# Streaming-encoder trunk on one core: statistics and transposes of q, k, v a slot later, last slab released by VectorE, high part of h by ScalarE

## What is computed

```python
def rms_norm(x, g):
    return x * lax.rsqrt(jnp.mean(x * x, axis=-1, keepdims=True) + EPS) * g

def odd_mixer(h, w_qkv, q_norm_g, k_norm_g, w_out):      # layer 1, 8 heads of 128
    q, k, v = jnp.split(h @ w_qkv, 3, axis=-1)
    q, k = rms_norm(q, q_norm_g), rms_norm(k, k_norm_g)  # per head
    o = stick_breaking(q, k, v)
    return o @ w_out

# per block of 128 queries, for all keys up to its end, mask: key < query
    z = q @ k.T * scale
    log_keep = where(mask, log_sigmoid(-z), 0)
    acc = cumsum(log_keep, reverse=True) - log_keep
    w = where(mask, exp(log_sigmoid(z) + acc), 0);  o = w @ v

# each layer l
    h = rms_norm(x, norm_mix_g[l]) * (1 + sc1) + sh1
    x = x + g1 * (even_mixer(h) if l % 2 == 0 else odd_mixer(h))
    h = rms_norm(x, norm_ffn_g[l]) * (1 + sc2) + sh2
    x = x + g2 * ((silu(h @ w_gate) * (h @ w_up)) @ w_down)
```

## Time and profile before

| | us |
|---|---|
| median of 3 runs | 2844.98 |
| the three runs | 2829.68, 2845.26, 2844.98 |
| the profiled execution | 2835.24 |
| its span (first to last instruction) | 2833.4 |
| PE busy in it | 2606.2 (92%) |
| DVE, ACT, POOL busy | 1412.3, 500.2, 973.7 |

### The profile page before, as it was taken

One profiled execution on the slowest core, in us unless ns is written; L12 is line 12 of the kernel. 1 busy time (PEld: TensorE's weight loads), 2 busy tenths in 40 slices (PEclk: granted clock), 3 DMA queues, 4 the chain that ended last, 5 costly groups with the idle time before them and its releaser, 6 DMA issues.

```text
span 2833.4 us, 35006 instructions
## 1 busy us (share of the span) xinstructions
PE 2606.2 (92%) x11394; PEld 2108.5 (74%) x11394; DVE 1412.3 (50%) x2207; ACT 500.2 (18%) x923; POOL 973.7 (34%) x1604
## 2 busy tenths in 40 slices
PE   2899889599999999999879999997899999999999
PEld 2687777487788888888657777775678888888887
DVE  5635666548434443334556776668482233333223
ACT  3001111111000000000126666565010000000001
POOL 1331222524444444445112222224064444334430
PEclk7799999799999999999979999998899999999999
DMA  6323333422222222222021011011311111111111
GB/s 223 112 92 117 91 95 104 146 92 68 82 81 75 74 74 74 74 74 89 23 82 31 31 38 34 30 30 56 126 45 53 52 52 50 47 44 44 52 37 60
DMA packets 216924, 201.87 MB, mean 71 GB/s; under 512 B 5994, under 2 KB 165892, under 8 KB 216708
## 3 DMA queue, kind: packets, MB, share of 16 engines
q1 hardware_dynamic: 202708, 164.13, 19.0%
q10 hardware_dynamic: 14128, 36.70, 3.5%
HBM read 179.84 MB, written 20.97 MB: 71 GB/s over the span
## 4 chain that ended last, share of the span: by engine, by line
PE 79%; DVE 11%; issue 3%; ACT 3%; DMA 2%; POOL 1%; SPq 0%; DVEq 0%; ACTq 0%; POOLq 0%
PE psG L551 23%; PE psG L556 23%; PE psG L557 23%; DVE n_t L1256 1%; PE psM L774 1%; ACT s_z L901 1%; DVE h_lo L1261 1%; DVE h_hi L1259 1%; PE psG L815 1%; DMA o_stg<-o_spill 1%; PE psO L551 1%; PE psZ L804 1%; DMA w_raw<-in_ev_w_in 1%; DVE n_sum L1235 1%; DVE r_w L1408 1%
## 5 line engine op out<-in xcount | busy, mean ns | idle before, releaser
L551 PE MATMUL psG<-h_hi,w_split 128*128 128x512 f32 x2496 | 998.6, 400 | 68.7 <-DVE h_lo L1193 34.3
L556 PE MATMUL psG<-h_lo,w_split 128*128 128x512 f32 x2496 | 984.9, 395 | 0.0
L557 PE MATMUL psG<-h_hi,w_split 128*128 128x512 f32 x2496 | 983.6, 394 | 0.0
L529 POOL TENSOR_SCALAR w_split<-w_raw 128x256 fp32r<-128x256 f32 x800 | 368.1, 486 | 1784.5 <-PE psG L551 640.8
L551 PEld LDWEIGHTS psG<-h_hi,w_split 128*128 128x128 f32 x2496 | 476.6, 191 | 192.3 <-issue 45.8
L533 POOL TENSOR_TENSOR w_split<-w_raw,w_split 128x256 fp32r<-128x256 f32 x800 | 614.0, 798 | 0.0
L557 PEld LDWEIGHTS psG<-h_hi,w_split 128*128 128x128 f32 x2496 | 476.1, 191 | 101.8
L556 PEld LDWEIGHTS psG<-h_lo,w_split 128*128 128x128 f32 x2496 | 477.4, 191 | 98.8 <-issue 3.0
L1458 DVE TENSOR_TENSOR hid<-sil,psG 128x512 f32<-128x512 f32 x88 | 60.6, 688 | 729.6 <-PE psG L557 729.5
L1468 DVE SCALAR_TENSOR_TENSOR xT<-psG,mod,xT 128x512 f32<-128x512 f32 x352 | 259.7, 748 | 167.0 <-PE psG L557 166.8
L901 ACT ACTIVATE sil<-psG 128x512 f32<-128x512 f32 x88 | 52.8, 600 | 1349.8 <-PE psG L557 1339.4
(11 more groups left out here) (160 smaller groups left out, 2120.2 us busy)
## 6 DMA issues: line engine op xcount, KB each, us to landing
ada_raw<-in_ada_w SPq DMA_DIRECT2D x80, 512.0 KB, 4.1
w_raw<-in_ffn_w_gate SPq DMA_DIRECT2D x44, 512.0 KB, 3.9
w_raw<-in_ffn_w_up SPq DMA_DIRECT2D x44, 512.0 KB, 3.8
w_raw<-in_ffn_w_down SPq DMA_DIRECT2D x44, 512.0 KB, 3.4
w_raw<-in_ev_w_in SPq DMA_DIRECT2D x28, 512.0 KB, 5.1
w_raw<-in_od_w_qkv SPq DMA_DIRECT2D x24, 512.0 KB, 3.8
ada_first<-in_ada_w SPq DMA_DIRECT2D x4, 2048.0 KB, 13.1
x_spill<-xT ACTq DMA_DIRECT2D x2, 4096.0 KB, 11.7
```

The costliest lines, as they stand in the source:

```text
L529: nc.gpsimd.tensor_scalar(slot[:, 0, part], raw[:, part], 1.0, 1.0, ALU.mult, ALU.mult).then_inc(hi_done, 1)
L551: mm = nc.tensor.matmul(o, st[0], mv[0], start=first, stop=False, **kw)
L556: nc.tensor.matmul(o, st[0], mv[1], start=False, stop=False, **kw)
L557: return nc.tensor.matmul(o, st[1], mv[0], start=False, stop=end, **kw)
```

## The change

Three parts.

First, in the heads: each element's pieces end in the slot named by the new DONE, in which ACT copies (and squares) it; PE's statistic or transposes, ACT's root or v's high part, and DVE's part now stand one slot later (TURNED), and within ACT's slot `second_step` comes ahead of `first_step`. The pieces are dealt out as 2, 2, eight times 1, and none in slots 0 and 11, in place of 2 and ten times 1.

Second, the last slab of a turn of the convolution and of a SwiGLU chunk is freed by DVE, right behind DVE's own wait for that step's gemm_done; PE no longer waits for its own matmul there. The output projections and the retention keep theirs.

Third, in the norms: there are two buffers n_t, ACT makes the high part (`norm_hi`, a pass of Identity with the shift as bias), and DVE makes n_t(k) and then the low part of tile k-1. In norm1 to norm3 ACT's high parts of half 0 stand between its squares of half 1, and those of half 1 follow the second root. In norm0 the spill of x (4 MB, one DMA of ACT's queue) stands ahead of all high parts and of the second root. The second root now waits for the last n_t of the first half and no longer for its last h_lo.

```diff
-PIECES = [0, 2, 1, 1, 1, 1, 1, 1, 1, 1, 1, 1]
-TAKEN = [2, 4, 6, 8, 10, NT]
-DONE = {t: e for e, t in enumerate(TAKEN)}
+PIECES = [0, 2, 2, 1, 1, 1, 1, 1, 1, 1, 1, 0]
+DONE = {t: e for e, t in enumerate([2, 3, 5, 7, 9, 11])}
+TURNED = {t + 1: e for t, e in DONE.items()}
...
-        n_t = at("n_t", N0 + 8 * KB, [H])
+        n_t = [at(f"n_t{n}", N0 + (8 + 2 * n) * KB, [H]) for n in range(2)]
...
@@ PE, convolution and SwiGLU @@
-                                used("conv", i, 6 * j + 3 + s, j == 1 and s == 2)
+                                if (j, s) != (1, 2):
+                                    used("conv", i, 6 * j + 3 + s)
...
-                            if h == 1 and m % 4 == 3:
-                                used(phase, i, 16 + m, m == 7)
+                            if h == 1 and m == 3:
+                                used(phase, i, 16 + m)
@@ PE, ACT, DVE, heads: stat, second_step, step @@
-                    if t in DONE:
-                        qkv_misc(phase, i, off, DONE[t], hd_next)
+                    if t in TURNED:
+                        qkv_misc(phase, i, off, TURNED[t], hd_next)
...
@@ ACT, slot @@
+                second_step()
                 first_step()
-                second_step()
@@ ACT, norms @@
+            def norm_hi(norm, h, k):
+                e = KT * (2 * int(norm[-1]) + h) + k
+                l, which = divmod(int(norm[-1]), 2)
+                sh = mod[:, l * MOD + 3 * KT * which + k:l * MOD + 3 * KT * which + k + 1]
+                act.wait_ge(n_ht, e + 1)
+                fn(hT[0][:, k, half(h)], n_t[k % 2][:], ACT.Identity, bias=sh).then_inc(n_hi, 1)
...
+                    for tile in tiles_after(k):
+                        norm_hi(norm, 0, tile)
...
                 if h:
-                    act.wait_ge(h_ready, KT * g)
+                    act.wait_ge(n_ht, KT * g)
...
-                for h in range(NH):
-                    norm_squares(norm, h, x_wait)
-                    norm_root(norm, h)
+                norm_squares(norm, 0, x_wait)
+                norm_root(norm, 0)
+                norm_squares(norm, 1, x_wait, lambda m: NORM_PLAN[1, m][1])
+                norm_root(norm, 1)
+                for k in range(KT):
+                    norm_hi(norm, 1, k)
@@ ACT, norm0 @@
-            norm_root("norm0", 1)
...
             spill("norm0", lambda: act.wait_ge(bank_read[3], 4))
+            for k in range(KT):
+                norm_hi("norm0", 0, k)
+            norm_root("norm0", 1)
+            for k in range(KT):
+                norm_hi("norm0", 1, k)
@@ DVE, norms @@
+                def low(self, h, k):
...
+                    dve.wait_ge(n_hi, e + 1)
+                    V.scalar_tensor_tensor(lo, n_t[k % 2][:], sh, hi.bitcast(F32), ALU.add, ALU.subtract).then_inc(h_ready, 1)
...
+                    if k >= 2:
+                        dve.wait_ge(h_ready, e - 1)
+                    V.scalar_tensor_tensor(n_t[k % 2][:], xT[:, k, half(h)], modA[:, 2 * l + which, k:k + 1], n_r[:], ALU.mult, ALU.mult).then_inc(n_ht, 1)
+                    if k:
+                        self.low(h, k - 1)
+                    if k == KT - 1:
+                        self.low(h, k)
@@ DVE, convolution and SwiGLU, behind dve.wait_ge(gemm_done, ...) @@
+                        if (j, h) == (1, 1):
+                            dve.sem_inc(slab_used, 1)
...
+                            if (h, m) == (1, KT - 1):
+                                dve.sem_inc(slab_used, 1)
```

More of the change, by code:

```diff
@@ L267, in build @@
         n_ht = sem("n_ht")
+        n_hi = sem("n_hi")
         h_ready = sem("h_ready")
@@ L904, in load_set, with norm_squares @@
                 nc.scalar.add_instruction(mybir.InstLoadActFuncSet(name=nc.get_next_instruction_name(), act_func_set_id=n))
-            def norm_squares(norm, h, x_wait):
+            def norm_hi(norm, h, k):
[4 more added lines that the diff above has]
+                fn(hT[0][:, k, half(h)], n_t[k % 2][:], ACT.Identity, bias=sh).then_inc(n_hi, 1)
+            def norm_squares(norm, h, x_wait, tiles_after=lambda m: ()):
                 g = 2 * int(norm[-1]) + h
@@ L1138, in second_step @@
                 def second_step(t):
-                    if t in DONE:
-                        qkv_second(phase, i, off, DONE[t], 1 - par, hd_next)
+                    if t in TURNED:
+                        qkv_second(phase, i, off, TURNED[t], 1 - par, hd_next)
                 for t in range(1, NT):
@@ L1239, in newton @@
                     g = 2 * self.q + h
+                    nt = n_t[0]
                     dve.wait_ge(n_rs, 2 * g + 2)
-                    V.scalar_tensor_tensor(n_t[:], psM[:], EPS, n_r[:], ALU.add, ALU.mult).then_inc(misc_read, 1)
+                    V.scalar_tensor_tensor(nt[:], psM[:], EPS, n_r[:], ALU.add, ALU.mult).then_inc(misc_read, 1)
                     dve.wait_ge(misc_read, norm_misc(self.norm, h))
-                    V.tensor_tensor(n_t[:], n_t[:], n_r[:], ALU.mult).then_inc(n_newt, 1)
+                    V.tensor_tensor(nt[:], nt[:], n_r[:], ALU.mult).then_inc(n_newt, 1)
                     dve.wait_ge(n_newt, 3 * g + 1)
-                    V.tensor_scalar(n_t[:], n_t[:], -0.5, 1.5, ALU.mult, ALU.add).then_inc(n_newt, 1)
+                    V.tensor_scalar(nt[:], nt[:], -0.5, 1.5, ALU.mult, ALU.add).then_inc(n_newt, 1)
                     dve.wait_ge(n_newt, 3 * g + 2)
-                    V.tensor_tensor(n_r[:], n_r[:], n_t[:], ALU.mult).then_inc(n_newt, 1)
+                    V.tensor_tensor(n_r[:], n_r[:], nt[:], ALU.mult).then_inc(n_newt, 1)
                     dve.wait_ge(n_newt, 3 * g + 3)
+                def low(self, h, k):
+                    l, which = divmod(self.q, 2)
+                    e = KT * (2 * self.q + h) + k
+                    sh = mod[:, l * MOD + 3 * KT * which + k:l * MOD + 3 * KT * which + k + 1]
+                    hi, lo = hT[0][:, k, half(h)], hT[1][:, k, half(h)]
+                    dve.wait_ge(n_hi, e + 1)
+                    V.scalar_tensor_tensor(lo, n_t[k % 2][:], sh, hi.bitcast(F32), ALU.add, ALU.subtract).then_inc(h_ready, 1)
                 def h_tile(self, h, k):
@@ L1253, in h_tile @@
                     e = KT * (2 * self.q + h) + k
-                    sh = mod[:, l * MOD + 3 * KT * which + k:l * MOD + 3 * KT * which + k + 1]
-                    dve.wait_ge(h_ready, e)
-                    V.scalar_tensor_tensor(n_t[:], xT[:, k, half(h)], modA[:, 2 * l + which, k:k + 1], n_r[:], ALU.mult, ALU.mult).then_inc(n_ht, 1)
-                    dve.wait_ge(n_ht, 2 * e + 1)
-                    hi, lo = hT[0][:, k, half(h)], hT[1][:, k, half(h)]
-                    V.tensor_scalar(hi, n_t[:], sh, None, ALU.add).then_inc(n_ht, 1)
-                    dve.wait_ge(n_ht, 2 * e + 2)
-                    V.scalar_tensor_tensor(lo, n_t[:], sh, hi.bitcast(F32), ALU.add, ALU.subtract).then_inc(h_ready, 1)
+                    if k >= 2:
[5 more added lines that the diff above has]
+                        self.low(h, k)
                 def after(self, h, m, plan):
@@ L1556, in step @@
                 def step(t):
-                    if t in DONE:
-                        qkv_dve(phase, i, off, DONE[t], 1 - par, hd_next)
+                    if t in TURNED:
+                        qkv_dve(phase, i, off, TURNED[t], 1 - par, hd_next)
                 for t in range(1, NT):
```

## The result

The changed kernel took 2767.61 us in the median of 4 runs (2762.85 to 2769.91), before 2845.12 in 4 (2829.68 to 2853.66): ratio 0.9731, interval 0.9687 to 0.9775. Repeated twice on later occasions beside other kernels it gave 2771.2 (0.9774, 0.9709 to 0.9838) and 2768.04 (0.9738, 0.9707 to 0.9769). The forecast had the direction and the order of the parts; with 2788 it stood 20 us above the median, and even the lower end of its range, 2769, stood 1.4 us above.

What follows compares the result with a forecast made beforehand. TensorE bounds the kernel, holding 79% of the chain of waits. Terms -23.3 - 4 - 10 - 9.5 - 4.3 - 0.5 = -51.6 took the profiled 2835.24 to 2783.6, plus 4.7 made 2788 us; range 2769 to 2813.

Steps and rivals of the forecast that it cites:

- Heads (-23.3 and -4): Seven attention heads: TensorE's waits shrink, 3.3 us per head, -23.3 in sum; a steadier clock gives another -4.
- z(2)'s 0.3: Boundary of heads: TensorE waits 0.3 us for z(2)'s weights, since slot 11 has no piece.
- A: Heads: waits only move; three-quarters of the 23.3 and the clock's 4 are lost, 2809 us; chance 0.13.
- B: Heads: the clock falls at every boundary, 15 us plus the 4, giving 2807 us; chance 0.09.
- C: Heads: ScalarE falls behind and stays behind, 1.1 us in nine slots of each head, 2867 us; chance 0.04.
- Slab release (-10): Convolution turns and SwiGLU chunks: VectorE frees the slab, TensorE doesn't drain; -10 us, ends -4 and -11.5.
- Rival D: Slab release: the next chunk's first matmul waits for its own slab or bank, no gain, 2798 us; chance 0.05.
- Norms (-9.5, -4.3, -0.5): Norm 0 -9.5 us, norm 2 -4.3, norms 1 and 3 together -0.5, with ScalarE making h's high part.
- Norm2's wait: Norm 2, half 1: the wait of 10.86 us for s_sq stays, since ScalarE does eight high parts first.
- the new wait for silu: Norms 1 and 3: first silu stands behind eight high parts on ScalarE, so TensorE waits; +1.45 us each.
- The base: Whole kernel: 4.7 us added because three runs of before had mean 2840.0 against the profiled 2835.24.
- The forecast's best ends together: Whole kernel: every term at its most favourable end, with the 4.7 added back, gives 2766 us.

Runs made afterwards that it cites:

- e1: Kernel before with only the heads' tables and order changed (first part alone): 2803.73 us, 0.9913 of before.
- e2: Kernel before with only the release of slabs by VectorE (second part alone): 2817.75 us, 0.9954 of before.
- g1: Changed kernel with TensorE again waiting for its own last matmul at the end of ffn1 chunks: a chunk takes 66.17 us, 0.89 more than without.
- e4: Kernel before with one wait added behind norm2: ScalarE's copy of element 0 waits for six tiles of the second half; 2832.11 us, 1.0002 of before.
- f2: Kernel before with one wait added behind norm2: ScalarE's copy of element 0 waits for five tiles of the second half; 2836.73 us, 1.0001 of before.
- f4: Changed kernel with the cast of the SwiGLU's hidden tile to its high part moved from VectorE to ScalarE: 2776.55 us, 0.9784 of before.
- g3: Changed kernel with element 1 using s_vsb for s_raw in the heads, and silu's table loaded earlier in norm1 and norm3: 2763.55 us, 0.9726 of before.
- g4: Changed kernel unaltered, run again for comparison on the same chip: 2768.04 us, 0.9738 of before.
- e3: Kernel before with only two n_t buffers, high part by ScalarE and early spill of x (third part alone): 2812.84 us, 0.9932 of before.
- f3: Changed kernel with other PIECES and DONE, so the elements in neighbouring slots are k's second half and v's first: 2788.3 us, 0.9841 of before.
- g2: Changed kernel with norm0's spill of x put back behind the second root, high parts ahead of it: 2767.0 us in one run.

## Why the prediction was right or wrong

**Heads (-23.3 and -4): right, and shown by e1.** The trace gave each wait: forecast 3.3 less per head, measured 65.22 to 61.65, 3.6; with the clock 29.2 in seven for 27.3. (3.3 x 7 is 23.1; the 23.3 has a rounding in it.) z(2)'s 0.3 is there as forecast. The rest is small change: v waits 0.2 less than forecast, and three of four statistics have their two matmuls 0.43 apart where it was 0.53 before. Against it stand 0.1 more at slot 4 and a new wait of 0.2 to 0.3 for s_w in the product with v. Rivals A and B, waits that only move and a clock that falls at each boundary, are out: the windows show 1.00, and e1 has the gain alone. C would have shown waits of 1.1 in nine slots; there is one of 0.64.

**Slab release (-10): the step that failed.** It measured 16.5 to 18.8 in e2, above its own upper end of 11.5. The mechanism was right, the size was not: I took the wait named in the earlier trace rows for the cost of the drain. The chunk itself was the better ruler: 288 matmuls at 0.2267 are 65.28, and before's chunk was 66.34. That is 1.06 instead of the named 0.76 in ffn1, and some 0.8 in an undisturbed chunk of ffn0 instead of the named 0.39, where I also left something to L602 that it didn't need. g1 shows the surplus of 0.3 over the named wait with the drain alone. What makes it wasn't tried. Rival D is out by e2.

**Norms (-9.5, -4.3, -0.5): mechanism right, the clock put at nothing without a reason.** Norm0's half 0 was forecast at 5 and gave 4.7 (means of profiles). Its half 1 gave 7.3 for 4.2: 0.7 from a tighter issue of tiles (1.45 against 1.57), and a remainder of 2.4 for the clock. (The forecast's own halves, 5 and 4.2 with 0 to 2 back for the spill, make 9.2 at most and not 9.5.) Norm2's wait stayed at 10.8 as forecast, and half 0 gave 5.0 for 4.3. The 3.0 behind it (2.1 in means) is the clock again, shown by e4, f2 and the step of 6.35. Norms 1 and 3 had the new wait for silu, 0.7 and 1.6 for 1.45 each.

**The base.** I added 4.7 to the sum because the first three runs of before lay above its profiled execution. The changed kernel's medians (2767.6, 2771.2, 2768.0) stand at its first profile's 2768.1. Larger samples of before have medians of 2830.8, 2834.2 and 2839.3, about the profiled 2835.2. So the addition wasn't borne out. With long passes of VectorE that cost 5 to 7 us each and come 0 to 2 times, a profile with one of them, as both of these are, was already a typical run.

So the 20.4 us are 6.5 to 8.8 of drains, 5.4 of clock in the norms, 1.4 of tiles and half 0 of norm2, 1.9 of heads and 4.7 of base, which is 19.9 to 22.2; what differs is chance and small stages. The result lies only just outside the range: of the two repetitions one (2771.2) is inside and one (2768.0) outside, and without the 4.7 of base all three would be inside. That part is luck; the size of the drains and the missing clock are not. The forecast's best ends together reached 2766, below its range, but they too were made of the named waits.

## What to carry to other kernels

Before pricing a drain of TensorE (a wait for its own last matmul) by its named wait, hold the period of the loop against its number of matmuls times their spacing: in ffn1 that difference, 1.06 us, is what went when the drain went. Where PE comes out of a long idle stretch, count the matmuls that follow at the low clock as well, and try to let them run while another engine's chain is under way; here one added wait made the stretch behind norm2 shorter. In a software pipeline, ask of each element by which slot its latest consumer wants it before moving it to loosen another pair.

## What the runs showed of the hardware

A single pass of VectorE took 5.5 to 6.6 us, in place of 0.43 or 0.69, while GpSimd split slabs without a break (ten or eleven passes of two kinds), and ended 0.3 to 0.6 after the last pass of a slab. It struck casts and, in f4, subtractions of two operands alike. Passes of over 5 us came only in ffn0; shorter ones of the kind came there too (1.7 to 3.0), in the convolution (3.0 to 3.2 in place of 0.5, in e2, g3 and g4) and in norm3 (2.1 in place of 0.69, in e3, f3, g2 and g3). The Trainium skill ("SBUF — State Buffer", "SBUF: two separate sides") tells of an exclusive lock between the two engines, held for one instruction; here the wait goes over ten of GpSimd's, so the measurement goes beyond that sentence.

An Identity of ScalarE with a bias from an operand took 724 ns (median of 64) where its Square took 632 on the same shape. The input is f32 in both; the output of the Identity is fp32r, that of the Square f32.

A drain of TensorE lengthened a loop of 288 matmuls by 0.89 us where the trace names a wait of 0.60 (g1), and by 1.06 where it names 0.76 (before).
